# The gate and up loop turned by one job, and the moved squares of a chunk taken up four slots later

## What is computed

```python
def swiglu(h, wg, wu, wd):
    return (jax.nn.silu(h @ wg) * (h @ wu)) @ wd
# D_MODEL = 2048, D_FF = 5632
x = x + 0.5 * swiglu(rmsnorm(x, ffn1_norm[i]), ffn1_wg[i], ffn1_wu[i], ffn1_wd[i])
x = x + hybrid_mixer(...)
x = x + 0.5 * swiglu(rmsnorm(x, ffn2_norm[i]), ffn2_wg[i], ffn2_wu[i], ffn2_wd[i])
```

## Time and profile before

| | |
|---|---|
| median of 3 runs | 1922.71 us (1921.33 to 1923.39) |
| the profiled execution, its own time | 1924.46 us |
| its span, first to last instruction | 1922.6 us |
| mean granted clock of TensorE | 0.996 |
| busy: PE, DVE, ACT, POOL | 99%, 53%, 47%, 11% |
| moved by DMA | 362.53 MB, 189 GB/s on average |

### The profile page before, as it was taken

One profiled execution on the slowest core, in us unless ns is written; L12 is line 12 of the kernel. 1 busy time (PEld: TensorE's weight loads), 2 busy tenths in 40 slices (PEclk: granted clock), 3 DMA queues, 4 the chain that ended last, 5 costly groups with the idle time before them and its releaser, 6 DMA issues.

```text
span 1922.6 us, 23375 instructions
## 1 busy us (share of the span) xinstructions
PE 1896.8 (99%) x8538; PEld 1546.3 (80%) x8539; DVE 1023.0 (53%) x1092; ACT 902.8 (47%) x1105; POOL 203.3 (11%) x376
## 2 busy tenths in 40 slices
PE   9999999999999999999999999999999999999998
PEld 7888888877888888887778778888887888888886
DVE  5545555445544444555665775455554555545444
ACT  6444444444444444444454545455444444444443
POOL 1111222111100000000000000111111111210000
PEclk9999999999999999999999999999999999999999
DMA  7666666666655556554335545656666666676554
GB/s 259 202 203 189 204 214 204 197 185 186 223 181 197 196 188 193 170 174 127 116 94 172 186 148 172 208 185 204 204 212 187 201 202 196 201 235 197 191 194 142
DMA packets 197213, 362.53 MB, mean 189 GB/s; under 512 B 18773, under 2 KB 23617, under 8 KB 197025
## 3 DMA queue, kind: packets, MB, share of 16 engines
q1 hardware_dynamic: 183264, 349.22, 57.7%
q0 software_dynamic: 11648, 12.02, 2.1%
q10 hardware_dynamic: 2240, 0.47, 0.1%
HBM read 348.01 MB, written 2.10 MB: 182 GB/s over the span
## 4 chain that ended last, share of the span: by engine, by line
PE 77%; POOL 7%; DVE 5%; DMA 4%; issue 4%; ACT 3%; ACTq 0%; POOLq 0%; DVEq 0%
PE ps L483 24%; PE ps L485 24%; PE ps L484 24%; POOL gu_raw L445 7%; DMA gu_raw<-gu_sq 4%; DVE w_lo L1180 2%; PE ps L504 2%; PE ps L643 1%; ACT w_hi L859 1%; DVE gu_sq L1242 1%; ACT L859 1%; PE ps L663 1%; DVE gu L1228 1%; PE ps L644 0%; PE ps L533 0%
## 5 line engine op out<-in xcount | busy, mean ns | idle before, releaser
L1180 DVE TENSOR_TENSOR w_lo<-raw,w_hi 128x1024 fp32r<-128x1024 f32 x656 | 791.3, 1222 | 617.6 <-ACT w_hi L859 616.6
L859 ACT ACTIVATE w_hi<-raw 128x1024 fp32r<-128x1024 f32 x656 | 683.9, 1059 | 672.5 <-PE ps L485 636.2
L483 PE MATMUL ps<-w_hi,hT_hi 128*128 128x512 f32 x1760 | 692.5, 393 | 12.4 <-DVE w_lo L1180 12.4
L485 PE MATMUL ps<-w_hi,hT_lo 128*128 128x512 f32 x1760 | 686.7, 390 | 0.0
L484 PE MATMUL ps<-w_lo,hT_hi 128*128 128x512 f32 x1760 | 686.5, 390 | 0.0
L483 PEld LDWEIGHTS ps<-w_hi,hT_hi 128*128 128x128 f32 x1760 | 331.6, 188 | 88.5 <-DVE w_lo L1180 18.9
L485 PEld LDWEIGHTS ps<-w_hi,hT_lo 128*128 128x128 f32 x1760 | 331.0, 188 | 69.6
L484 PEld LDWEIGHTS ps<-w_lo,hT_hi 128*128 128x128 f32 x1760 | 331.4, 188 | 67.1
L445 POOL DMA_DIRECT2D gu_raw<-gu_sq x352 | 187.7, 542 | 893.7 <-DVE gu_sq L1242 816.0
L483 PE MATMUL ps<-w_hi,guT_hi 128*128 128x512 f32 x704 | 274.3, 390 | 0.0
L485 PE MATMUL ps<-w_hi,guT_lo 128*128 128x512 f32 x704 | 274.0, 389 | 0.0
(11 more groups left out here) (196 smaller groups left out, 813.1 us busy)
## 6 DMA issues: line engine op xcount, KB each, us to landing
raw<-in_ffn_wg_dram SPq DMA_DIRECT2D x176, 512.0 KB, 4.5
raw<-in_ffn_wu_dram SPq DMA_DIRECT2D x176, 512.0 KB, 4.8
raw<-in_ffn_wd_dram SPq DMA_DIRECT2D x176, 512.0 KB, 4.5
raw<-in_w_in_dram SPq DMA_DIRECT2D x88, 512.0 KB, 3.6
raw<-in_w_out_dram SPq DMA_DIRECT2D x32, 512.0 KB, 3.8
gu_raw<-gu_sq POOLq DMA_DIRECT2D x352, 32.0 KB, 4.4
raw<-in_cmp_k_w_dram SPq DMA_DIRECT2D x8, 256.0 KB, 3.5
raw<-in_cmp_v_w_dram SPq DMA_DIRECT2D x8, 256.0 KB, 4.3
```

The source lines that it names most:

```text
L483: mm(o, x_hi, w_hi[:, s, kk, :], start=first and kk == 0, stop=False)
L485: ins = mm(o, x_lo, w_hi[:, s, kk, :], start=False, stop=last and kk == GK - 1)
L859: act.activation(w_hi[:, c % SLOTS, :, :], raw[:, c % SLOTS, :, :], ACT.Copy).then_inc(hi_ready, 1)
L1180: tt(w_lo[:, s, :, :], raw[:, s, :, :], w_hi[:, s, :, :].bitcast(F32), ALU.subtract).then_inc(lo_ready, 1)
```

## The change

In each FFN the up job of chunk 0 is taken out ahead of the loop. A pass of the loop is now the gate job of chunk i + 1 and then the up job of chunk i + 1, and no up job is left behind it. The sequence of groups, loads and matmuls is the same as before. On every one of PE, ACT, DVE and SP the jump back now stands between an up job and a gate job, where it stood between a gate job and an up job.

The second part is `GU_AT` = 3. `gu_operand` of chunk i now stands after slot 3 of the up job of chunk i + 1, on ACT and on DVE, where it stood after slot 7 of the gate job of chunk i + 1: four slots later. For the last chunk it goes from slot 8 to slot 11 of the first down job, and `vectors` on ACT, in the first FFN, from slot 10 to slot 14. Since `gu_operand` no longer stands between the squares of one chunk and the silu of the next, ACT's `silu` gets a wait of its own on `gu_squares`, before it writes `gu` again.

```diff
+GU_AT = 3
 ...
@@ sync @@
+                for j in range(JD):
+                    load(c + j, wu[f][:, GK * j:GK * j + GK, 0:CH])
+                c += JD
                 with sp.Fori(0, NFC - 1) as i:
                     for j in range(JD):
-                        load(c + j, wu[f][:, GK * j:GK * j + GK, bass.ds(i * CH, CH)], i, 2 * JD)
+                        load(c + j, wg[f][:, GK * j:GK * j + GK, bass.ds(i * CH + CH, CH)], i, 2 * JD)
                     for j in range(JD):
-                        load(c + JD + j, wg[f][:, GK * j:GK * j + GK, bass.ds(i * CH + CH, CH)], i, 2 * JD)
+                        load(c + JD + j, wu[f][:, GK * j:GK * j + GK, bass.ds(i * CH + CH, CH)], i, 2 * JD)
                 c += 2 * JD * (NFC - 1)
-                for j in range(JD):
-                    load(c + j, wu[f][:, GK * j:GK * j + GK, (NFC - 1) * CH:FF])
-                c += JD
@@ tensor @@
-                with pe.Fori(0, NFC - 1) as i:
-                    job(c, JD, hT_hi, hT_lo, 1, i, 2 * JD)
-
-                    pe.wait_ge(silu_done, count(2 * (NFC * f + 1), i, 2))
-                    job(c + JD, JD, hT_hi, hT_lo, 0, i, 2 * JD)
-
-                    pe.wait_ge(gu_done, count(2 * (NFC * f + 1), i, 2))
-                c += 2 * JD * (NFC - 1)
                 job(c, JD, hT_hi, hT_lo, 1)
                 c += JD
+                with pe.Fori(0, NFC - 1) as i:
+                    pe.wait_ge(silu_done, count(2 * (NFC * f + 1), i, 2))
+                    job(c, JD, hT_hi, hT_lo, 0, i, 2 * JD)
+                    pe.wait_ge(gu_done, count(2 * (NFC * f + 1), i, 2))
+                    job(c + JD, JD, hT_hi, hT_lo, 1, i, 2 * JD)
+                c += 2 * JD * (NFC - 1)
@@ scalar, silu @@
+                if n or i is not None:
+                    act.wait_ge(gu_squares, count(NFC * f + n, i, 1))
@@ scalar, ffn @@
+                job(c, JD, after={1: [lambda: silu(f, 0, c)]})
+                c += JD
                 with act.Fori(0, NFC - 1) as i:
-                    job(c, JD, i, 2 * JD, after={1: [lambda: silu(f, 0, c, i)]})
-                    job(c + JD, JD, i, 2 * JD, after={JD - 1: [lambda: gu_operand(f, 0, i)]})
+                    job(c, JD, i, 2 * JD)
+                    job(c + JD, JD, i, 2 * JD, after={1: [lambda: silu(f, 1, c + JD, i)],
+                                                      GU_AT: [lambda: gu_operand(f, 0, i)]})
                 c += 2 * JD * (NFC - 1)
-                job(c, JD, after={1: [lambda: silu(f, NFC - 1, c)]})
-                c += JD
                 for n in range(NDC):
                     if n == 0:
-                        after = {JD: [lambda: gu_operand(f, NFC - 1)]}
+                        after = {JD + GU_AT: [lambda: gu_operand(f, NFC - 1)]}
                         if f == 0:
-                            after[10] = [vectors]
+                            after[14] = [vectors]
@@ vector, ffn @@
-                with dve.Fori(0, NFC - 1) as i:
-                    job(c, JD, i, 2 * JD)
-                    job(c + JD, JD, i, 2 * JD, after={1: [lambda: up(f, 0, c + JD, i)],
-                                                      2: [lambda: gu_transpose(f, 0, i)],
-                                                      JD - 1: [lambda: gu_operand(f, 0, i)]})
-                c += 2 * JD * (NFC - 1)
                 job(c, JD)
                 c += JD
+                with dve.Fori(0, NFC - 1) as i:
+                    job(c, JD, i, 2 * JD, after={1: [lambda: up(f, 0, c, i)], 2: [lambda: gu_transpose(f, 0, i)]})
+                    job(c + JD, JD, i, 2 * JD, after={GU_AT: [lambda: gu_operand(f, 0, i)]})
+                c += 2 * JD * (NFC - 1)
 ...
-                                 JD: [lambda: gu_operand(f, NFC - 1)]}
+                                 JD + GU_AT: [lambda: gu_operand(f, NFC - 1)]}
```

## The result

The change made the kernel faster: 1903.03 us, median of 4 runs (1902.96 to 1903.06), against 1922.94 (1921.33 to 1923.39, now four runs as well). The ratio is 0.9898, 95% interval 0.9881 to 0.9915. The prediction was 1903.0 us, range 1900.5 to 1908.0. On a second chip the changed kernel took 1903.07 and the kernel before 1920.67, ratio 0.9914 (0.9897 to 0.993).

What follows compares the result with a forecast made beforehand. PE, busy 99%, was taken as the bound, losing time only in waits for `w_lo`: 8.35 + 8.48 + 0.80 + 0.95 + 1.72 = 20.3 us. Off the 1922.71 median that gives 1902.4, put at 1903.0; range 1900.5 to 1908.

Steps and rivals of the forecast that it cites:

- eighteen waits: PE's weight loads wait for DVE's `w_lo` at the up job's start, nine per FFN; all were to go.
- 0.9 us of cover: At the up job's start, lead left without the 1.28 us table load, which turns it into 0.4 of wait.
- The late passes: Two passes where PE stood 3.69 and 2.74 us; POOL started late in one, landing 20.6 after gate start; both waits go.
- due time of 25.2: Operand's new place after up slot 3: due 25.2 us after the gate job's start, 7.9 to spare ordinarily, 4.6 late.
- 3.7 of cover: Behind the operand's new place, the next group's low part is ready 3.7 us before PE wants it.
- PE's lead of 3.7 us: At the loop's jump, PE's 0.207 us jump was done 3.7 us before the gate job's last matmul; priced at nothing.
- The sum: Both FFN loops: 20.3 us lost to waits and a clock fall, 1.13 for each of 18, all to be won.
- small waits: Waits that couldn't be named, no place given; forecast put a little above 1902.4, at 1903.0.
- the jump shows: Rival at PE's loop jump: no longer hidden behind a wait for DVE, 3.7 us come back, about 1906.7; 10%.
- a fetch at each jump: Rival at the loop jumps: code fetched again, costing 9 or 75 us, low end about 1912; 3%.
- The part-gain by crowding: Rival in the up job: its third or fifth group takes over the small wait, 9 to 10 us won, about 1912; 6%.
- The slower rival: Rival at the operand's new place: squares land too late; at 14 us later PE stands 2.4 in 18 passes, 1946; 4%.

Runs made afterwards that it cites:

- one silu ahead: Kernel before, with a one-column silu on ACT ahead of each FFN's loop, operand not moved: 1907.19 us, against 1918.54 for the kernel before.
- behind G6: Changed kernel with the operand after slot 6 of the gate job, one group earlier than before the change: 1944.02 us, ratio 1.0116 to the kernel before.
- the run with the operand behind U0: Changed kernel with GU_AT = 0, the operand after slot 0 of the up job: 1903.43 us, against 1918.54 for the kernel before.
- the written-out loops: Changed kernel with the gate and up loops written out on all five engines, so none jumps: 1902.31 us, against 1903.07 for the changed kernel.
- the run with ten additions: Changed kernel with ten 128x512 additions on POOL, each waited for, ahead of each chunk's sixteen issues: 2049.56 us, ratio 1.0677 to the kernel before.
- the run with eight small loads: Kernel before, with eight more loads of 16 rows issued by POOL at the start: 1919.01 us, ratio 1.0 to the kernel before.
- the turn alone: Changed kernel with the operand put back after slot 7 of the gate job, loop still turned: 1906.80 us, against 1918.54 for the kernel before.

## Why the prediction was right

**The bound.** PE was the bound except for eighteen waits, and nothing else took their place. The pace of 43.52 a pass held: from the first operand of the loop on ACT to the tenth, 81.14 to 472.82 in the trace after, are nine passes, 391.68 us or 43.52 each.

**The ordinary pass.** The prediction took from two crossings that 0.9 us of cover was left without the table load. With the loads taken out and the operand's wait left, sixteen waits became two small ones. That step was right, and a reader could have drawn more from it: one line outside the loop gives most of the gain.

**The reach.** How late the squares may land can be read from each of PE's waits in the loops: it is the landing, counted from the gate job's start (0.2 before the product on DVE), less the wait. Two rows of before that go with the earlier trace rows:

```profile
210.50 0.19 PEld L483 LDWEIGHTS ps<-w_hi,hT_hi 128*128 128x128 f32 x1 [0.64 <-DVE w_lo L1180]
...
409.89 1.41 DVE L1228 SCALAR_TENSOR_TENSOR gu<-ps,rs,gu 128x512 f32<-128x512 f32 x2 [3.23 <-PE ps L485]
```

Before, it is 205.76 - 188.48 - 0.60 = 16.7 in the ordinary pass and 430.04 - 409.69 - 3.65 = 16.7 in the late one, and 16.7 in all eighteen. With one silu ahead it is 424.30 - 405.27 - 1.23 = 17.8, behind G6 15.1, behind U3 28.7, each the same in every pass with a wait. So each group later gives one group's time, 2.72 (17.8 + 4 x 2.72 = 28.7), and the table load at the loop's head took 1.1. Ordinary squares landed near 17.3: 0.6 beyond the first figure and 0.5 within the second. The prediction had 0.9 of cover and the load at its full 1.28; both are a little too large, and in the wait of an ordinary pass the two errors nearly cancel.

**The late passes.** By the product on DVE the squares landed 20.3 after the gate job's start in the first late pass, and not 20.6; the prediction counted the start from the earlier trace rows there. Against a due time of 25.2 it makes no difference. That 3.7 of cover was left behind the due time is confirmed by the reach of 28.7, and the due time by the run with the operand behind U0: 14.7 there, and 14.7 + 4.0 is the landing of 18.8 to within 0.1.

**The jump.** Priced at nothing from PE's lead of 3.7 us, and between the marks it is nothing.

**The sizes.** The sum was 20.3; the two FFNs gave 19.9. The first FFN was put at 8.35 + 0.80 + 1.72 = 10.9 and gave 10.6, the second at 9.4 and gave 9.3. The span fell by 21.4 because the fall of the clock in the mixer, 1.6, was in the first of these two traces only; the prediction had named no such term. It looked for a span near 1902.3, and 1901.2 came. The median fell by 19.9 on the first chip, 17.6 on the second. The prediction took the loss of one profiled run, which lay 1.75 above the median, off that median, and had 1902.4. It then added 0.6 for small waits; the trace after has none in the loops, so nothing shows this term. That the two together met 1903.03 to the hundredth is luck. That the time lay within the range is not, for the time without waits was the same on both chips; but the way there, by the loss, is the weaker one. Taken from the median of the second chip, the same sum would have given 1900.4, just outside the range.

**The rivals.** That the jump shows, and a fetch at each jump, are out by the written-out loops and by the empty instruction queues of the changed kernel. (In the stretch of the earlier trace rows PE had its eight jumps; ACT and DVE had seven.) The part-gain by crowding is out by the timeline. The slower rival exists, but PE begins to stand only some 11.5 us beyond where ordinary squares land. Its price was too low: the new place stands in 20 passes and not 18, and the falls of the clock behind waits of that size were left out.

## What to carry to other kernels

A wait costs nothing until the lead is used up, and from there on each further tenth in the chain is paid by the engine that bounds the kernel. So look for the cheapest link (here a table load of 1.28 us) and not for the longest wait (5.2 us). Before a loop, put the engine's state (the table set) to what the loop leaves behind; the compiler then had nothing to reload in each pass here (9 loads in place of 47). And predict the time that is left when the waits are gone, from the pace of the bounding engine: it was more stable here (1903.03 and 1903.07 on two chips) than the time of the kernel that waits (medians from 1918.46 to 1922.94).

## What the runs showed of the hardware

- POOL's arithmetic slows DVE. One `w_lo`, 1.22 us in the mean elsewhere, took 2.04 while POOL added (in the run with ten additions), and over that run the mean of the 656 went from 1222 to 1338 ns. The Trainium skill, "GPSIMD Engine Reference", section "Specifications", says that the two share interfaces to the memory and contend when DVE has two inputs there, as `w_lo` has; the trace agrees, with these numbers. POOL's transfer issues did not show it.
- POOL's first issue of a move was 3.1 us late (7.5 us behind the product in place of 4.4, without additions) at the 9th and the 17th of 22 moves, in every trace. The cause is open.
- A fall of TensorE's clock to 1.2 GHz came at each of the twenty waits of 3.8 to 6.2 us in the loops of the run with ten additions, and behind those of 3.69 and 2.74 us in the trace of before. Behind waits of 2.3 to 2.8 us it came in some cases and not in others: 2.59 us in the run with eight small loads and 2.76 behind G6 had none, 2.30 behind G6 had one. Behind the waits of 1.27 to 1.64 us in the runs with one silu ahead and with the turn alone the granted clock stayed at 1.00. In the mixer a fall came in eight of fourteen traces, at the same place.
- A table load took 1.28 us on ACT, and the next instruction began 0.02 us behind its end.
